# A two-layer diffusion backbone: a third modulation unit ahead of the first attention pair, four late slices in the last one

## The reference

```python
sh_m, sc_m, g_m, sh_f, sc_f, g_f = jnp.split(silu(c) @ ada_w[i] + ada_b[i], 6)   # per layer; also for c_ctx
hx = modulate(rmsnorm(x), sh_m, sc_m)            # layer 0 does the same for ctx
# layer 0: low-rank latents, 8 heads, keys of context and latents together
q_lat, kv_lat, k_rope = split(hx @ mla_w_in)
x = x + g_m * (attend(q, k, v) @ mla_w_out)
# layer 1: x = x + g_m * short_conv_mixer(hx)
# both layers: 16 experts, each takes its 64 best tokens
x = x + g_f * ec_moe(modulate(rmsnorm(x), sh_f, sc_f))
```

## Time and profile before

| what | value |
|---|---|
| median of 3 runs | 1592.2 us (1591.47 to 1592.33) |
| profiled execution | 1592.2 us |
| its span, first to last instruction | 1590.4 us |
| mean granted TensorE clock | 0.98 of full |
| busy: TensorE, VectorE, ScalarE | 91%, 42%, 15% |
| HBM read | 497.6 MB, 317 GB/s over the span |
| low-rank tiles begin | 38.3 us |
| first pair begins | 124.1 us |
| last pair begins, ends | 304.7 us, 348.2 us |
| layer 0's experts begin | 439.9 us |

### The profile page before, as it was taken

One profiled execution on the slowest core, in us unless ns is written; L12 is line 12 of the kernel. 1 busy time (PEld: TensorE's weight loads), 2 busy tenths in 40 slices (PEclk: granted clock), 3 DMA queues, 4 the chain that ended last, 5 costly groups with the idle time before them and its releaser, 6 DMA issues.

```text
span 1590.4 us, 15656 instructions
## 1 busy us (share of the span) xinstructions
PE 1454.8 (91%) x6490; PEld 678.2 (43%) x6490; DVE 668.4 (42%) x1161; ACT 232.3 (15%) x430; POOL 80.5 (5%) x72
## 2 busy tenths in 40 slices
PE   4999999999599999999989899999599999998987
PEld 2655656554233333332323588854133333333332
DVE  2576777433713232322322778734423232232223
ACT  3133453333300000000000300013100000000000
POOL 0010010000000000000000033000100000000000
PEclk9999999999889999999999999999699999999999
DMA  9933221496589999999999923452699999999996
GB/s 383 339 120 118 82 104 53 166 391 269 198 344 426 427 426 427 426 428 427 426 427 428 388 71 108 165 218 107 246 428 427 425 427 428 426 427 427 427 427 293
DMA packets 59248, 504.93 MB, mean 317 GB/s; under 512 B 7999, under 2 KB 8222, under 8 KB 29482
## 3 DMA queue, kind: packets, MB, share of 16 engines
q1 hardware_dynamic: 54928, 490.69, 75.1%
q0 software_dynamic: 2752, 8.92, 1.5%
q10 hardware_dynamic: 1498, 4.33, 0.7%
HBM read 497.62 MB, written 6.29 MB: 317 GB/s over the span
## 4 chain that ended last, share of the span: by engine, by line
PE 72%; DMA 20%; DVE 5%; ACT 2%; issue 1%; ACTq 0%; DVEq 0%; POOLq 0%
PE ps L1011 31%; DMA work<-in_exp_w_up_dram 11%; PE ps L1095 9%; PE ps L870 7%; DMA ring<-in_exp_w_up_dram 6%; PE ps L1027 5%; PE ps L617 3%; PE ps L777 3%; PE ps L736 3%; PE ps L679 2%; PE ps L675 2%; PE ps L740 1%; PE ps L763 1%; DMA work<-in_ada_w_dram 1%; PE ps L1049 1%; PE ps L995 1%
## 5 line engine op out<-in xcount | busy, mean ns | idle before, releaser
L1011 PE MATMUL ps<-ring,work 128*64 128x512 f32 x1824 | 409.2, 598 | 31.2 <-ACT work L1355 13.0
L1011 PE MATMUL ps<-work 128*64 128x512 f32 x1248 | 282.5, 601 | 20.9 <-ACT work L1355 8.9
L1890 DVE TENSOR_TENSOR work<-ps,work 128x1024 f32<-128x1024 f32 x120 | 141.3, 1219 | 283.1 <-PE ps L1027 283.1
L1011 PEld LDWEIGHTS ps<-ring,work 128*64 128x64 f32 x1824 | 127.5, 137 | 294.2 <-issue 250.4
L1011 PEld LDWEIGHTS ps<-work 128*64 128x64 f32 x1248 | 87.4, 138 | 202.2 <-issue 172.1
L1027 PE MATMUL ps<-work 64*128 64x512 f32 x480 | 119.3, 615 | 0.0
L1908 DVE SCALAR_TENSOR_TENSOR work<-ps,gate_e,gate_ffn 128x512 f32<-128x512 f32 x32 | 24.0, 751 | 185.8 <-PE ps L1011 185.8
L1901 DVE TENSOR_TENSOR work<-work,ps 128x512 f32<-128x512 f32 x32 | 22.0, 687 | 176.1 <-issue 151.8
L1351 ACT ACTIVATE work<-ps 128x512 f32<-128x512 f32 x32 | 19.1, 597 | 487.3 <-PE ps L1011 487.3
L2078 POOL DMA_INDIRECT work<-xn_rows,row_no x32 | 30.6, 956 | 1036.5 <-PE ps L995 733.2
L1355 ACT ACTIVATE work<-ps 128x512 f32<-128x512 f32 x32 | 19.1, 597 | 372.8 <-PE ps L1049 372.8
(11 more groups left out here) (306 smaller groups left out, 1355.3 us busy)
## 6 DMA issues: line engine op xcount, KB each, us to landing
ring<-in_exp_w_gate_dram SPq DMA_DIRECT2D x38, 2048.0 KB, 31.7
ring<-in_exp_w_up_dram SPq DMA_DIRECT2D x37, 2048.0 KB, 32.4
ring<-in_exp_w_down_dram SPq DMA_DIRECT2D x37, 2048.0 KB, 33.6
work<-in_exp_w_up_dram SPq DMA_DIRECT2D x27, 2048.0 KB, 31.5
work<-in_exp_w_gate_dram SPq DMA_DIRECT2D x24, 2048.0 KB, 34.8
work<-in_exp_w_down_dram SPq DMA_DIRECT2D x23, 2048.0 KB, 36.8
ring<-in_ada_w_dram SPq DMA_DIRECT2D x32, 1024.0 KB, 7.0
ring<-in_ada_w_dram SPq DMA_DIRECT2D x6, 2048.0 KB, 7.6
```

The source lines that it names most:

```text
L1011: last = mm(PS[64 * h:64 * h + 64, bank, :], lhsT[:, m * P + 64 * j:m * P + 64 * j + 64], slot_rows[sl][:, m, h * BANK:(h + 1) * BANK], st ...
L1890: v.tensor_tensor(row, PS[:, b:b + 2, :], row, ALU.add).then_inc(added[L], 1)
```

## The change

Five things, all in the part ahead of the experts of layer 0:

- Transposes 6 and 7 move from ahead of the first low-rank tile into it, after its fourth row block; banks are assigned anew (`T_BANKS`).
- `UNITS_IN` becomes `[3, 0, 0, 0, 3]`, and there are 6 units. Unit 2 runs ahead of the first pair, from a third buffer in R[1]; the third pair has none. The gate's sum there waits for the projection copy.
- The last pair has units 3, 4 and 5 (rows 0 to 3 of group 4 are units 4 and 5). Unit 3 uses buffer 0, units 4 and 5 both use buffer 1.
- Rows 4 to 7 of group 4 become four slices in `late_w`, W[0:8192]. Their loads stand behind the units' loads in SyncE's stream; `add_late` runs on VectorE in the last pair, the first ahead of its first maximum; their sum stands in the mixer's first tile, bank 7, and VectorE adds it to `ada_part[0]`.
- Expert chunks 0 and 1, which used to be loaded to W[0:8192] in the last pair, are loaded behind that sum.

```diff
+        ada_buf = [view(t, lo, 2, GROUP) for t, lo in ((R[2], 0), (R[2], 2 * GROUP), (R[1], 0))]
+        late_w = [view(W, n * GROUP, GROUP) for n in range(4)]
-        T_BANKS = [0, 1, 3, 6, 4, 5]
+        T_BANKS = [4, 5, 0, 1, 3, 6, 0, 1]
-        UNITS_IN = [2, 0, 0, 1, 5]
+        UNITS_IN = [3, 0, 0, 0, 3]
-        UNIT_BANK = [2, 0, 7] + [7, 6, 7, 7, 7]
+        UNIT_BANK = [2, 0, 1, 7, 6, 7]
+        UNIT_BUF = [0, 1, 2, 0, 1, 1]
@@ block.sync
             for n in range(UNITS):
-                if n == GATE_AT:
+                if n == 3:
                     for m in range(KC):
                         if m < 4:
-                            sp.wait_ge(unit_mm, m // 2 + 1)
+                            sp.wait_ge(unit_mm, (1, 1, 2, 3)[m])
...
-                elif n == GATE_AT + 1:
+                elif n == 4:
                     sp.wait_ge(gate_mm, 1)
-                elif n >= 2:
-                    sp.wait_ge(unit_mm, n - 1)
+                elif n == 5:
+                    sp.wait_ge(unit_mm, n)
...
             sp.wait_ge(proj, 10 * PAIRS)
-            load_chunk(0, 0)
-            load_chunk(0, 1)
+            for m in range(4):
+                sp.dma_start(late_w[m], ada_w[1, (4 + m) * P:(5 + m) * P, 2 * D:4 * D]).then_inc(ada_in[m], 16)
             for h, done in ((0, mixw_in[0]), (1, out_half_in)):
-                sp.wait_ge(unit_mm, UNITS - 1 + h)
+                sp.wait_ge(unit_mm, (4, 6)[h])
...
-            for n in (2, 3, 4, 5, 9):
+            for n in (2, 3, 4, 5):
+                load_chunk(0, n)
+            sp.wait_ge(ada_main, FIRST_LOADS + 3)
+            for n in (0, 1, 9):
                 load_chunk(0, n)
@@ block.tensor
             ada_collect(0)
-            for g in range(6, KC):
-                input_T(g)
...
                 if n == 0:
+                    pe.wait_ge(inT_a, 1)
+                    pe.wait_ge(inT_d, 1)
+                if n == 1:
                     pe.wait_ge(inT_a, 3)
                     pe.wait_ge(inT_d, 3)
...
                     for k in range(KC):
+                        if n == 0 and lo == 0 and k == 4:
+                            input_T(6)
+                            input_T(7)
...
                     if i == 2:
-                        pe.wait_ge(unit_added, u + 1)
+                        pe.wait_ge(proj_d, 5 * (i + 2))
                         gate_sum(0, gate_w[1][:, 3, :], 7)
...
-                    unit(u + 3)
                     scores(3)
                     probs_T(2)
-                    unit(u + 4)
...
                     if t == 0:
                         constant()
+                        if L == 0:
+                            pe.wait_ge(unit_added, UNITS)
+                            slices_sum(2 * KC + 4, late_w[3], 7)
@@ block.vector
+            def add_late(m):
+
+                dve.wait_ge(ada_in[m], 16 * (part_loads(4 + m) + 1))
+                if m == 0:
+                    ins = v.tensor_scalar(late_w[0], late_w[0], cond_T[:, 4, 0:1], None, ALU.mult)
+                else:
+                    dve.wait_ge(slice_added, 2 * KC + m)
+                    ins = v.scalar_tensor_tensor(out=late_w[m], in0=late_w[m], scalar=cond_T[:, 4 + m, 0:1], in1=late_w[m - 1],
+                                                 op0=ALU.mult, op1=ALU.add)
+                ins.then_inc(slice_added, 1)
...
                 for t in range(XT):
+                    if i == PAIRS - 1 and t == 0:
+                        add_late(0)
...
-                    if not ahead:
+                    if not ahead and t < 2:
                         add_unit(u + t + 1)
+                    if not ahead and t < 3:
+                        add_late(t + 1)
...
                 add_mix(0, 1)
+                if L == 0:
+                    dve.wait_ge(ada_main, FIRST_LOADS + 3)
+                    v.tensor_tensor(ada_part[0], PS[:, 7, :], ada_part[0], ALU.add).then_inc(ada_rows, 1)
```

More of the change, by code:

```diff
@@ L67, in build @@
     GROUPS = [((0, 0), (0, 1)), ((0, 2), (0, 3)), ((0, 4), (1, 4)), ((1, 0), (1, 1)), ((1, 2), (1, 3))]
-    UNITS = (len(GROUPS) - 3) * KC // 2
+    UNITS = 6
     assert VD == P and D == FF == 2 * BANK and T == BANK and CAP * 2 == P and D == KC * P and LAT == QL + KVL + ROPE
@@ L159, in build @@
         mla_out = [view(R[2], h * KC * BANK, KC, BANK) for h in range(2)]
-        ada_buf = [view(R[2], h * 2 * GROUP, 2, GROUP) for h in range(2)]
+        ada_buf = [view(t, lo, 2, GROUP) for t, lo in ((R[2], 0), (R[2], 2 * GROUP), (R[1], 0))]
         ada_acc = R[0][:, 0:GROUP]
         ada_slice = [R[0][:, m * GROUP:(m + 1) * GROUP] for m in (1, 2, 3)]
+        late_w = [view(W, n * GROUP, GROUP) for n in range(4)]
         part_w = [view(R[2], n * GROUP, GROUP) for n in range(4)]
@@ L274, in build @@
         gate_in, gate_added, gate_mm = [sem("gate_in0"), sem("gate_in1")], sem("gate_added"), sem("gate_mm")
-        unit_in = [sem("unit_in0"), sem("unit_in1")]
+        unit_in = [sem("unit_in0"), sem("unit_in1"), ada_in[3]]
         ada_main, ada_rows, ada_sum, ada_out, mod_ready = (sem(n) for n in (
@@ L320, in part_loads, with unit_loads @@
         def part_loads(k):
-            return (4, 4, 3, 1)[k % 4] + k // 4 + 1
+            return (4, 4, 3, 3)[k % 4] + k // 4 + 1
+        def unit_loads(n):
+            return 32 * sum(UNIT_BUF[m] == UNIT_BUF[n] for m in range(n + 1)) + 16 * (UNIT_BUF[n] == 2)
         def unit_of(n):
@@ L420, in _ @@
                 for kk in range(2):
-                    rows, buf = slice((2 * kp + kk) * P, (2 * kp + kk + 1) * P), ada_buf[n % 2][:, kk, :]
+                    rows, buf = slice((2 * kp + kk) * P, (2 * kp + kk + 1) * P), ada_buf[UNIT_BUF[n]][:, kk, :]
                     if L == other:
-                        sp.dma_start(buf, ada_w[L, rows, lo * D:lo * D + GROUP]).then_inc(unit_in[n % 2], 16)
+                        sp.dma_start(buf, ada_w[L, rows, lo * D:lo * D + GROUP]).then_inc(unit_in[UNIT_BUF[n]], 16)
                     else:
                         sp.dma_start(buf.rearrange("p (l n) -> p l n", l=2), ada_w[:, rows, lo * D:(lo + 1) * D].rearrange("l p n -> p l n")
-                                     ).then_inc(unit_in[n % 2], 16)
+                                     ).then_inc(unit_in[UNIT_BUF[n]], 16)
             def load_chunk(L, n):
@@ L530, in ada_product, with slices_sum @@
                 ada_slices(ADA_BANK, first_ada[u], 2 * u, u == 0, u == FIRST_LOADS - 1).then_inc(ada_main, 1)
-            def slices_sum(c, acc_w, bank):
-                pe.wait_ge(slice_added, c * KC)
+            def slices_sum(slices, acc_w, bank):
+                pe.wait_ge(slice_added, slices)
                 for g in range(4):
@@ L566, in input_T @@
             def input_T(g):
-                b = T_BANKS[g % 6] if g < KC else 6 + g % 2
+                b = T_BANKS[g] if g < KC else 6 + g % 2
                 if 6 <= g < KC:
-                    pe.wait_ge((inT_a, inT_d)[g % 2], 1)
+                    pe.wait_ge((inT_a, inT_d)[g % 2], 2)
                 if g == KC:
@@ L645, in unit @@
             def unit(n):
-                pe.wait_ge(unit_in[n % 2], 32 * (n // 2 + 1))
+                pe.wait_ge(unit_in[UNIT_BUF[n]], unit_loads(n))
                 if n == 1:
@@ L656, in unit @@
                     pe.wait_ge(unit_added, n - 1 if n == UNIT_AT[PAIRS] + 1 else n)
-                ada_slices(UNIT_BANK[n], ada_buf[n % 2], 2 * unit_of(n)[1], True, True).then_inc(unit_mm, 1)
+                ada_slices(UNIT_BANK[n], ada_buf[UNIT_BUF[n]], 2 * unit_of(n)[1], True, True).then_inc(unit_mm, 1)
             def project(n, s, units):
@@ L800, in pair @@
                         pe.wait_ge(proj_d, 5 * (i + 2))
-                        slices_sum(2, part_w[3], 7)
+                        slices_sum(2 * KC, part_w[3], 7)
                     if UNITS_IN[i + 1]:
@@ L839, in _ @@
                 if s == 5:
-                    slices_sum(1, ada_acc, ADA_BANK)
+                    slices_sum(KC, ada_acc, ADA_BANK)
             pe.wait_ge(ada_rows, 2)
@@ L845, in _ @@
             turn(0, range(0, 3))
-            for n in range(2):
+            for n in range(UNITS_IN[0]):
                 unit(n)
@@ L977, in mixer_out @@
                     pe.wait_ge(sq, XT)
+                    pe.wait_ge(ada_rows, 4)
                     ada_collect(PAIRS - 1)
@@ L1171, in _ @@
                 act.wait_ge(inT, g + 1)
-                f(hT[:, g, CX:KEYS], PS[:, T_BANKS[g % 6], :], ACT.Identity, bias=modv[0][0][:, 0, g, 0:1],
+                f(hT[:, g, CX:KEYS], PS[:, T_BANKS[g], :], ACT.Identity, bias=modv[0][0][:, 0, g, 0:1],
                   scale=scl[0][0][:, g, 0:1]).then_inc(inT_a, 1)
@@ L1436, in _ @@
                 dve.wait_ge(inT, g + 1)
-                v.tensor_scalar(hT[:, g, CX:KEYS], PS[:, T_BANKS[g % 6], :], scl[0][0][:, g, 0:1], modv[0][0][:, 0, g, 0:1],
+                v.tensor_scalar(hT[:, g, CX:KEYS], PS[:, T_BANKS[g], :], scl[0][0][:, g, 0:1], modv[0][0][:, 0, g, 0:1],
```

1 line of the change is left out of this document (removed).

## The result

The changed kernel takes 1606.66 us in the median of 4 runs (1605.16 to 1607.58), the kernel before 1591.84 us in 4 runs beside it. The ratio is 1.0091, 95% interval 1.0078 to 1.0104: 14.8 us slower. The forecast was 12.5 us slower, 1604.7 us, in a range from 1600.0 to 1609.0.

What follows compares the result with a forecast made beforehand. TensorE was taken to bound the kernel (72% of the chain of waits, DMA 20%). From 1592.2 us, 0 − 2.1 − 1.9 + 15.5 + 1.0 = +12.5 us gave 1604.7 us, range 1600 to 1609.

Steps and rivals of the forecast that it cites:

- A: First low-rank tile placed around transposes 6 and 7: same work behind the same wait, 0 us, bounds 0.5 either way.
- B: Third unit ahead of the first attention pair: shorter idle gap keeps full clock for the scores, −2.1 us (other end +0.6).
- C: Third attention pair without its unit: TensorE saves that unit's time, −1.9 us.
- Rival 1: Before the first pair, the 1.4 us gap still drops the clock: +0.6 there, +15.2 in all, 1607.4 us; chance 0.30.
- D: Last pair: late-slice stall +13.7, half clock behind it +3.0, two units gone −1.2; together +15.5 us.
- E: Late slices' sum in the mixer's first tile, where TensorE has no gap: +1.0 us.
- F: Expert chunks 0 and 1 loaded behind the late sum: still in time before the experts, 0 us.
- The prediction's last sign: If all waits are as said but the total is not, the cause lies in the experts, taken to move as a block.

Runs made afterwards that it cites:

- e1: Changed kernel with the four late-slice loads issued ahead of SyncE's wait for unit 4; 1592.67 us, ratio 0.9999 to the kernel before.
- e6: Kernel before with only transposes 6 and 7 moved into the first low-rank tile, banks as in the change; 1592.37 us, ratio 0.9999.
- e5: Kernel before with only rows 4 to 7 of group 4 as late slices, loaded early, and six units; 1592.46 us, ratio 0.9999.
- e2: Changed kernel with each late addition one query tile later on VectorE, loads left where they are; 1598.52 us, ratio 1.0042 to the kernel before.

## Why the prediction was right, and where it was off

- **The direction and the place:** right, and for the reason given. One TensorE wait of 13.37 us (forecast 13.7) between unit 4 and the second scores, caused by the order of SyncE's queue. e1 moved nothing else and the 14 us were gone.
- **A, forecast 0:** measured 0.0 us alone (e6). Inside the trace the first tile waits for VectorE's eviction instead of ScalarE's, 0.2 us later than before.
- **B, forecast −2.1: the step that failed.** I took the row of the 2.20 us gap with a clock of 1.00 as the price of such a gap, and concluded that a 1.4 us one would keep it. The new gap was 1.81 us; the clock was kept in five of seven traces, so the place was read rightly for most traces. But one row was one trace: behind that same gap the clock fell in five of ten, and it stayed in the kernel. In all four traces in which the first gap passed without a fall and the second was there, the second one had it: −1.77 and then +1.70 in the first trace. The step booked a gain at one gap and took the next one, of the same kind, as free. The medians agree that B brings about nothing: in e1 the other terms sum to −0.2 us (−2.0 for C, −1.2 for the units, +1.8 for unit 5's loads, +1.2 in the mixer and at the experts), and −0.1 us was measured (interval −1.6 to +1.3); with −2.1 for B it would be −2.3. Why the clock falls behind some of these gaps and not others stays open.
- **Rival 1** (+0.6 for B, 1607.4 us in all) came nearer to the measured 1606.66 us than the forecast, but partly by luck: its mechanism, a fall behind the first gap, was there in two of seven traces.
- **C, forecast −1.9:** −1.97.
- **D, forecast +15.5:** +15.05. Wait 13.4 for 13.7, clock 2.9 for 3.0, units −1.2 as forecast, split −0.1 and −1.1 (waits of 1.66 and 0.69 us where they had stood). A unit of 1.9 us that fills a wait of 1.66 us is worth 0.1, one that fills 0.69 us is worth 1.1: the sum that counts only TensorE's work would have put −3.7 there.
- **E, forecast +1.0:** 0.9 us for the sum. The stretch grew by 1.25 us; the other 0.35 us lie in the wait in front of the first expert matmul, 1.40 us for 1.05, in every kernel with late slices, also in e5. It was not in the sum, and its cause stays open.
- **F, forecast 0:** no wait on a chunk in the mixer or at the first expert in any trace.
- **The total:** 12.5 forecast, 14.8 measured between the medians, 15.2 between the two traced spans. In the two traces the stretches of the forecast's terms (−1.77, −1.97, +15.05, +1.25) sum to 12.6, which is the forecast. What is left is +1.70 behind the second gap, which is B's error, +1.64 at the start, mostly chance, and −0.70 from the first expert on. The prediction's last sign failed here: all waits were as said and the total was not, and yet the experts moved as a block to within 0.7 us; the difference stood ahead of them.
- **The Trainium skill's advice** (TensorE: Matmul & The Clock Gate, Part 1), to leave the ramp uncounted at under 1% of a span, would have given +12.2. That is only 0.3 us from the forecast, because what it adds at B (+0.6 for −2.1, that is 2.7) and what it takes off D (3.0) nearly cancel, so the total does not decide between the two sums; the trace does, place by place. The 2.9 us behind the stall are indeed 0.2% of this span; but they are a fifth of what the change did, and the 1.7 us (projection, 5.37 for 3.67) to 2.1 us (first scores, 4.97 for 2.82) of a single fall decide whether part B is a gain. For the difference of two close kernels it has to be counted.

## What to carry to other kernels

When work moves from one way of loading to another, write down the issuing queue in order and ask, for each new load, which wait stands in front of it and which engine runs into its landing: a load behind a wait on a buffer inherits that wait, however long its own space has been free. An addition ahead of the instruction that a softmax chain begins with costs its load's whole delay, here a TensorE wait of 13.4 us; one place later the waits came to 5.8 us. And a wait that is filled elsewhere has to be followed to the next wait of the same kind before its clock is booked as a gain.

## What the runs showed of the hardware

- The granted clock is not a function of the kernel alone. The same 2.23 us TensorE wait was followed by full clock (projection 3.67 us) in five traces and by half clock (5.37 us) in five, and which it was differed between two traces of one kernel.
- A fall came behind waits far shorter than the long one: behind 1.81 us in two of seven traces, behind 2.59 us in all five. The cost was 1.4 to 2.6 us in the block behind it.
- After a 4.05 us wait (e2) the block of scores took 5.49 us, exactly as after 13.37 us: between these two, the length of the wait did not add to the price of the fall.
- Loads of 1 MB from one queue landed in the order of issue, 4.7, 6.9 and 8.9 us after their own issues for three issued within 0.85 us, so the third landed 9.8 us after the first issue; a bundle 220 us earlier, in the kernel before, had 10.0.
